# Attention by pairs of heads: scale in the queries, mask and maximum in one operation, reciprocals on a diagonal

## The reference

```python
s_nb  = einsum(q_r, k_nb) * dh**-0.5 + bias          # neighbourhood: bias, or -1e30 off the window
s_ctx = einsum(q_r, kc)   * dh**-0.5
probs = softmax(concat([s_nb, s_ctx]))
out   = einsum(probs_nb, v_nb) + einsum(probs_ctx, vc)
# windowed GQA: the same with a band mask, q heads 4g..4g+3 on kv head g, and a sink:
probs = softmax(concat([s_band, s_ctx, s_sink]))     # the sink has no value row
```

## Time and profile before

| | us |
|---|---|
| median of 3 runs | 3332.6 (3328.14 to 3336.45) |
| the profiled execution | 3334.65 |
| its span | 3332.8 |
| mean granted clock of TensorE, share of 2.4 GHz | 0.76 |
| TensorE (PE) busy | 2535.4 (76%) |
| VectorE (DVE) busy | 1962.9 (59%) |
| ScalarE (ACT) busy | 515.1 (15%) |
| GpSimd (POOL) busy | 973.9 (29%) |
| moved from HBM and to it | 1023.45 MB, mean 307 GB/s |

### The profile page before, as it was taken

The page is one execution under the profiler, slowest core; times in us unless marked ns, Lnnn a source line. Parts: engine busy times, 40 slices in busy tenths (PEclk is TensorE's granted clock), DMA queues, the critical chain, the costliest instruction groups (busy, mean ns, idle before and its releaser), DMA issues.

```text
span 3332.8 us, 32715 instructions
## 1 busy us (share of the span) xinstructions
PE 2535.4 (76%) x10880; PEld 1289.2 (39%) x10880; DVE 1962.9 (59%) x6008; ACT 515.1 (15%) x1106; POOL 973.9 (29%) x967
## 2 busy tenths in 40 slices
PE   6889983789999969658889876777988366566555
PEld 5768872243455535124444411113677011111111
DVE  4778958747544466875444455554646855555555
ACT  2151111124322111002022200001502000000000
POOL 0830000276322222323932233331000233333332
PEclk7989986695899979668889866566898555665666
DMA  7606732897899979886999999994042599989997
GB/s 301 234 29 260 300 132 112 342 380 277 349 400 377 384 297 368 323 339 256 334 388 402 410 362 398 393 401 196 26 160 95 228 372 388 407 343 403 403 405 309
DMA packets 147881, 1023.45 MB, mean 307 GB/s; under 512 B 18816, under 2 KB 19328, under 8 KB 28032
## 3 DMA queue, kind: packets, MB, share of 16 engines
q0 software_dynamic: 110592, 805.36, 60.9%
q1 hardware_dynamic: 30496, 202.36, 15.9%
q10 hardware_dynamic: 6624, 13.64, 1.1%
HBM read 1011.32 MB, written 9.96 MB: 306 GB/s over the span
## 4 chain that ended last, share of the span: by engine, by line
PE 45%; DMA 20%; DVE 19%; POOL 8%; issue 5%; ACT 3%; ACTq 0%; DVEq 0%; POOLq 0%; SPq 0%
DMA ring<-in_peer_uv,eT 20%; PE PS L1043 10%; PE PS L821 6%; DVE ring L1709 6%; POOL ring L660 5%; PE PS L978 5%; PE PS L1061 4%; PE PS L756 3%; PE PS L939 2%; PE PS L842 2%; PE PS L826 2%; PE PS L885 2%; PE PS L908 2%; DVE ring L1379 1%; POOL mix L555 1%
## 5 line engine op out<-in xcount | busy, mean ns | idle before, releaser
L1709 DVE CUSTOM_DVE_ANT_0 ring<-ring,PS 128x512 f32<-128x512 f32 x1536 | 993.2, 684 | 830.1 <-PE PS L1061 454.8
L660 POOL DMA_INDIRECT ring<-in_peer_uv,eT x768 | 726.6, 946 | 2224.0 <-PE PS L1043 1339.7
L1061 PE MATMUL PS<-xr,onesb 3*128 3x512 bf16 x1536 | 610.4, 483 | 379.1 <-DVE hcol L1709 329.1
L1043 PE MATMUL PS<-ring,zcol 128*32 128x512 f32 x3072 | 601.0, 924 | 185.9 <-DVE zcol L1719 184.6
L1061 PEld LDWEIGHTS PS<-xr,onesb 3*128 3x128 bf16 x1536 | 108.8, 96 | 959.1 <-DVE hcol L1709 474.6
L1043 PEld LDWEIGHTS PS<-ring,zcol 128*32 128x32 f32 x3072 | 104.8, 144 | 491.5 <-DVE zcol L1719 257.2
L821 PE MATMUL PS<-uT,W 128*128 128x256 f32 x1024 | 249.9, 393 | 4.3 <-issue 4.3
L1312 ACT ACTIVATE ge<-hdot 128x4 f32<-128x4 f32 x192 | 39.4, 205 | 1382.7 <-DVE hdot L1714 1371.4
L1379 DVE CUSTOM_DVE_ANT_0 ring<-ring 128x1024 f32<-128x1024 f32 x160 | 211.6, 1361 | 28.6 <-DMA ring<-in_w_rows 23.8
L821 PEld LDWEIGHTS PS<-uT,W 128*128 128x128 f32 x1024 | 193.5, 194 | 62.8 <-issue 34.7
L978 PE MATMUL PS<-uT,W 128*128 128x256 f32 x768 | 183.2, 395 | 0.0
(11 more groups left out here) (190 smaller groups left out, 2418.9 us busy)
## 6 DMA issues: line engine op xcount, KB each, us to landing
ring<-in_w_rows SPq DMA_DIRECT2D x40, 1024.0 KB, 8.0
W<-in_w_in SPq DMA_DIRECT2D x30, 1024.0 KB
W<-in_w_q SPq DMA_DIRECT2D x24, 1024.0 KB
W<-in_w_gate SPq DMA_DIRECT2D x16, 1408.0 KB
W<-in_w_gate SPq DMA_DIRECT2D x16, 1280.0 KB
W<-in_w_gate SPq DMA_DIRECT2D x16, 1024.0 KB
W<-in_w_out SPq DMA_DIRECT2D x12, 1024.0 KB
xr<-xrows ACTq DMA_DIRECT2D x768, 6.0 KB
```

Source lines behind the costliest of these rows:

```text
L660: pool.indirect_dma_start(ring[:, slot, :], None, (peer_uv0, peer_uv1)[b.l], bass.IndirectOffsetOnAxis(eT[:, f % 2, t:t + 1], 0)).then_inc ...
L1043: last = T.matmul(PS[k * NR:(k + 1) * NR, (6 + h) * 512:(7 + h) * 512], zcol[:, g % 2, k, NR - 1 - at:2 * NR - 1 - at], ring[:, slot, D + ...
L1061: T.matmul(bank(x_bank(q, n) + h), onesb[32 * k:32 * k + 3, :], xr[32 * k:32 * k + 3, g % 2, h * 512:(h + 1) * 512], start=True, stop=True)\
L1709: V.tensor_tensor_reduce(out=u_half, in0=u_half, in1=bank(x_bank(q, n) + h), scale=1.0, scalar=0.0, op0=ALU.mult, op1=ALU.add, accum_out=h ...
```

## The change

The 24 jobs become 12 of two heads each, one on each half of the partitions. The scale goes into the queries when they leave PSUM (`qcols` holds the scaled bias columns, made once at the start). `bounded` takes the place of `scaled`: one `tensor_tensor_reduce` for each 256 columns adds the mask (or a zero) and takes the row's maximum, writing the scores to `Sm` with the accumulator. `normed` no longer scales the rows; it writes the reciprocals onto two 128x128 diagonals in `stage_c` (identity times reciprocal), and `transposed` is an ordinary product of the scores with that diagonal. `Sm` is 2 pairs deep, so that `bounded(n)` waits for `transposed(n-2)`; `PT` moves to `mix`. The latent scores alternate between banks 2, 3 and 6, 7; the context's have banks 2 and 3 alone, and `scores(n+1)` there waits for the maximum of pair n. Step n holds `transposed(n-1)` and `values(n-2)`, 14 steps instead of 27, with a share of 2.0 tokens each instead of 1.2. ScalarE does `exps` ahead of `probs` and `outputs`. GpSimd issues two taps of the convolution a step. The heads of `w_branch_d` are laid out in the new order on the host.

```diff
-SHARE = {"ada": 1.0, "ln": 1.5, "unit": 0.9, "fft": 0.9, "rope": 1.2, "job": 1.2, "conv": 1.3, "gate": 1.1, "out": 0.9,
+SHARE = {"ada": 1.0, "ln": 1.5, "unit": 0.9, "fft": 0.9, "rope": 1.2, "job": 2.0, "conv": 1.3, "gate": 1.1, "out": 0.9,
...
-    return [(br, h, qt) for br, heads in ((0, NAT_H), (1, GQA_H)) for h in range(heads) for qt in range(TT)]
+    return [(br, c, qt) for br, pairs in ((0, NAT_H // 2), (1, GQA_H // 2)) for c in range(pairs) for qt in range(TT)]
...
-        Sm = part(scr, 0, [SM, 2 * TOK])
-        PT = part(scr, SM * 2 * TOK, [2 * TOK])
+        Sm = part(scr, 0, [2, 2, 2 * TOK])
+        PT = part(mix, 14 * TOK, [4 * TOK])
...
+        def s_bank(s, n):
+            return 6 if s == 0 and n % 2 else 2
...
-                for n in range(len(JOBS) + 3):
+                for n in range(len(JOBS) + 2):
+                    next(taps[b.front], None)
                     next(taps[b.front], None)
...
+                    br, c, qt = JOBS[n]
+                    at = s_bank(s, n)
+                    before = 2 if s == 0 else 1
+                    if n >= before:
+                        pe.wait_ge(a["sm"], a.at("sm", n - before + 1))
+                    rows_ = [slice(e * DH, (e + 1) * DH) for e in range(2)]
+                    of_q = (nq, gqk)[br]
...
+                        ks = [nkb[st_][:, c, :] for st_ in ((0, 1) if s == 0 else (1,))]
...
+                        ks = [gqk[:, 4, :], gkc[:, :]] if s == 0 else [gkc[:, :]]
                     for m, k_ in enumerate(ks):
-                        last = T.matmul(bank(2 + n % 2, m * TOK, (m + 1) * TOK), q_, k_, start=True, stop=True)
+                        for e in range(2):
+                            last = T.matmul(bank(at + e, m * TOK, (m + 1) * TOK), of_q[rows_[e], c, qt * P:(qt + 1) * P],
+                                            k_[rows_[e], :], start=True, stop=True)
                     last.then_inc(a["S"], 1)
...
-                    for q in range(nk):
-                        last = T.transpose(bank(4, q * P, (q + 1) * P), Sm[:, n % SM, q * P:(q + 1) * P], ident[:, :])
+                    for e in range(2):
+                        for q in range(nk):
+                            to = bank((4, 0)[e], q * P, (q + 1) * P) if s == 0 else bank(4, (2 * e + q) * P, (2 * e + q + 1) * P)
+                            last = T.matmul(to, Sm[:, n % 2, e, q * P:(q + 1) * P], stage_c[:, n % 2, e * P:(e + 1) * P],
+                                            start=True, stop=True)
                     last.then_inc(a["ptp"], 1)
...
+                        st_ = (0, 0, 1, 1)[q] if s == 0 else 1
+                        for e in range(2):
+                            if br == 0:
+                                v_ = nvf[st_][:, q % 2, (2 * c + e) * DH:(2 * c + e + 1) * DH]
+                            else:
+                                v_ = gvb[st_][:, q % 2, e * DH:(e + 1) * DH]
+                            last = T.matmul(PS[e * DH:(e + 1) * DH, 5 * 512:5 * 512 + P], v_,
+                                            PT[:, (e * nk + q) * P:(e * nk + q + 1) * P], start=(q == 0), stop=(q == nk - 1))
...
                 scores(0)
-                for n in range(len(JOBS) + 3):
+                for n in range(len(JOBS) + 2):
                     if n + 1 < len(JOBS):
                         scores(n + 1)
-                    if 2 <= n < len(JOBS) + 2:
-                        transposed(n - 2)
-                    if n >= 3:
-                        values(n - 3)
+                    if 1 <= n <= len(JOBS):
+                        transposed(n - 1)
+                    if n >= 2:
+                        values(n - 2)
...
+                        if dst[0] in ("nq", "gq"):
+                            j = dst[1] + 2 * (dst[0] == "gq")
+                            A(dst_of[dst[0]](dst[1]), bank(2 + n % 4, 0, TOK), fn, scale=SCALE, bias=qcols[:, l, j:j + 1])\
+                                .then_inc(a["unit_act"], 1)
...
                     act.wait_ge(a["sm"], a.at("sm", n + 1))
-                    last = A(Sm[:, n % SM, 0:w], Sm[:, n % SM, 0:w], ACT.Exp, bias=st8[:, q, 1:2], accum_out=st8[:, q, 2:3])
+                    for e in range(2):
+                        last = A(Sm[:, q, e, 0:w], Sm[:, q, e, 0:w], ACT.Exp, bias=st[:, q, 4 + e:5 + e],
+                                 accum_out=st[:, q, 6 + e:7 + e])
                     if br:
-                        last = A(st8[:, q, 3:4], sink[:, h:h + 1], ACT.Exp, bias=st8[:, q, 1:2])
+                        last = A(st[:, q, 8:10], st[:, q, 8:10], ACT.Exp)
...
-                    A(PT[:, 0:w], bank(4, 0, w), ACT.Copy).then_inc(a["pts"], 1)
+                    if s == 0:
+                        A(PT[:, 0:w], bank(4), ACT.Copy)
+                        A(PT[:, w:2 * w], bank(0), ACT.Copy).then_inc(a["pts"], 1)
+                    else:
...
-                for n in range(len(JOBS) + 3):
-                    if 2 <= n < len(JOBS) + 2:
-                        probs(n - 2)
-                    if n >= 3:
-                        outputs(n - 3)
+                    A(yb[:, (2, 6)[br] + c, qt * P:(qt + 1) * P], bank(5, 0, P), ACT.Copy).then_inc(a["y"], 1)
+                act.wait_ge(pch_s, gated[b.front])
+                for n in range(len(JOBS) + 2):
                     if n < len(JOBS):
                         exps(n)
+                    if 1 <= n <= len(JOBS):
+                        probs(n - 1)
+                    if n >= 2:
+                        outputs(n - 2)
...
-                def scaled(n):
...
-                    if n >= SM:
-                        dve.wait_ge(a["ptp"], a.at("ptp", n - SM + 1))
+                    if n >= 2:
+                        dve.wait_ge(a["ptp"], a.at("ptp", n - 1))
+                    go = dict(scale=1.0, scalar=LOWEST, op0=ALU.add, op1=ALU.max)
+                    none = zero[:, 0:1].to_broadcast([P, TOK])
+                    for e in range(2):
+                        if s == 0:
+                            m_ = bias[:, qt, 2 * c + e, :] if br == 0 else band[:, qt, :]
+                            ch.add(V.tensor_tensor_reduce(out=Sm[:, q, e, 0:TOK], in0=bank(at + e, 0, TOK), in1=m_,
+                                                          accum_out=st[:, q, e:e + 1], **go))
+                        ch.add(V.tensor_tensor_reduce(out=Sm[:, q, e, w - TOK:w], in0=bank(at + e, w - TOK, w), in1=none,
+                                                      accum_out=st[:, q, 2 + e:3 + e], **go))
+                    ch.wait()
...
-                        m_ = bias[:, qt, h, :] if br == 0 else band[:, qt, :]
-                        ch.add(V.scalar_tensor_tensor(Sm[:, n % SM, 0:TOK], bank(b_, 0, TOK), SCALE, m_, ALU.mult, ALU.add))
-                        ch.link(V.tensor_scalar(Sm[:, n % SM, TOK:w], bank(b_, TOK, w), SCALE, None, ALU.mult))
+                        ch.link(V.tensor_tensor(st[:, q, 2:4], st[:, q, 0:2], st[:, q, 2:4], ALU.max))
+                    if br:
+                        of_c = sink[:, c:GQA_H:GQA_H // 2]
+                        ch.link(V.tensor_tensor(st[:, q, 2:4], st[:, q, 2:4], of_c, ALU.max))
+                        ch.link(V.tensor_scalar(st[:, q, 4:6], st[:, q, 2:4], -1.0, None, ALU.mult))
+                        V.tensor_tensor(st[:, q, 8:10], of_c, st[:, q, 4:6], ALU.add).then_inc(a["sm"], 1)
                     else:
-                        ch.link(V.tensor_scalar(Sm[:, n % SM, 0:w], bank(b_, 0, w), SCALE, None, ALU.mult))
-                    ch.link(V.reduce_max(st8[:, q, 0:1], Sm[:, n % SM, 0:w], AX))
-                    if br:
-                        ch.link(V.tensor_tensor(st8[:, q, 0:1], st8[:, q, 0:1], sink[:, h:h + 1], ALU.max))
-                    V.tensor_scalar(st8[:, q, 1:2], st8[:, q, 0:1], -1.0, None, ALU.mult).then_inc(a["sm"], 1)
+                        V.tensor_scalar(st[:, q, 4:6], st[:, q, 2:4], -1.0, None, ALU.mult).then_inc(a["sm"], 1)
...
-                        ch.link(V.tensor_tensor(st8[:, q, 2:3], st8[:, q, 2:3], st8[:, q, 3:4], ALU.add))
-                    ch.link(V.reciprocal(st8[:, q, 4:5], st8[:, q, 2:3]))
-                    V.tensor_scalar(Sm[:, n % SM, 0:w], Sm[:, n % SM, 0:w], st8[:, q, 4:5], None, ALU.mult).then_inc(a["pn"], 1)
-                for n in range(len(JOBS) + 3):
+                        ch.link(V.tensor_tensor(st[:, q, 6:8], st[:, q, 6:8], st[:, q, 8:10], ALU.add))
+                    ch.link(V.reciprocal(st[:, q, 10:12], st[:, q, 6:8]))
+                    for e in range(2):
+                        last = V.tensor_scalar(stage_c[:, q, e * P:(e + 1) * P], ident[:, :], st[:, q, 10 + e:11 + e], None,
+                                               ALU.mult)
+                        if e:
+                            last.then_inc(a["pn"], 1)
+                        else:
+                            ch.add(last)
```

More of the change, by code:

```diff
@@ L260, in build @@
         ge = sb("ge", [P, 2, GRP])
-        st8 = sb("st8", [P, 2, 8])
+        st = sb("st", [P, 2, 12])
```

(2 more changed lines are left out.)

62 lines of the change are left out of this document (27 added, 35 removed).

## The result

| | before | changed |
|---|---|---|
| median of 4 runs | 3334.5 us (3328.1 to 3340.8) | 3376.4 us (3368.3 to 3379.5) |
| ratio | | 1.0121, 95% interval 1.0098 to 1.0144 |

A forecast was written before the change was run, and what follows sets the result against it. TensorE was taken to bound all three attentions before, and the wait loop through VectorE and the transposes the changed latent ones. -6.5 - 9 + 4 + 7 = -4.5 on 3334.65 gave 3330 us, median 3328; range 3303 to 3358.

The forecast's parts named there:

- Prices of a pair: Latent attention, full clock: reads 0.35 us each, transposes 1.95 to 2.05, scores 1.05 and values 1.0 with halves overlapping.
- The rivals without overlap: Products on array halves don't overlap: pairs at all (3370 us, chance 0.14) or only the values (3340 us, 0.08).
- a rival with the values at 2.0: Only the values don't overlap, TensorE's latent cycle 4.9 us, total 3340 us; chance 0.08.
- The cycle of the latent attention: Reads wait for the transposes of pair n-1, making a loop of 4.45 us, or 5.05 with a sink.
- Lead-in, half clock and tail of the latent attentions: Latent attentions: lead-in 7.4 us at full clock, tail 2.2, half clock +4.3 in the first, +5 in the third.
- -6.5: First latent attention: 68.5 us for 75.0.
- -9: Second latent attention (third of the three attentions): 68.5 us for 77.5.
- At full clock ... mean 8.3: Context attention: mean step 8.3 us at full clock for 3.5 steps, against 10.85 at half clock for 9.
- +4: Context attention: 127 us against 123, with three quarters of the time at half clock.
- "They fall into its idle time, 0" to "+7": Selection: 5 more tokens at 1.4 to 1.6 us each add 7 us, or 0 if VectorE's idle time takes them.
- The rival that ended slower: Pairs don't overlap on the array: +12 us in each latent attention, +18 in the context, total 3370 us; chance 0.14.
- The sign that was named for "wrong": Latent cycles near 5.8 or 8 us; context attention under 115 or over 140 us.

The follow-up runs named there:

- experiment 8: Changed kernel, but in the latent attentions VectorE does reciprocals and diagonals of pair n-1 ahead of the reads of pair n: 3354.3 us, ratio 1.0051.
- Experiment 7: Context attention in half steps, TensorE's next scores moved behind the first token, two pairs deep: 3351.4 for 3374.1 us; moved ahead of it, three deep: 3346.8 for 3329.0.
- share_2_3: Changed kernel with the share of a job step 2.3 instead of 2.0, putting 32 tokens into the context attention: 3367.3 us, ratio 1.0087.
- share_0: Changed kernel with the share of a job step 0, so no tokens in the context attention: 3370.2 us (one run).

## Why the prediction was wrong

It said 3330 us for the profiled execution; its own time is 3379.5, 49 us more. By its own steps:

- **Prices of a pair: right.** Reads 0.35 apart, eight scores 1.13 for 1.05, transposes 2.05 as said, sixteen values 1.09 for 1.0, and both products overlap on halves of the array. The rivals without overlap fall. The rule of the Trainium skill ("TensorEngine Tiling (Array Packing)", Key Properties) that different tiles run in parallel agrees with this trace. From the rule of the Trainium skill on weight loads ("TensorE: Matmul & The Clock Gate", Part 3, What overlaps and what doesn't) the prediction had drawn a rival with the values at 2.0; they took 1.09.
- **The cycle of the latent attention: right in its mechanism, a little low in size.** 5.30 for 5.05 in seven cycles, 4.41 in the last. It was rightly read that reads wait for transposes; experiment 8 shows it.
- **Lead-in, half clock and tail of the latent attentions: too small.** By the terms of the sum, each to the end of its transposes, for the first attention: lead-in 12.1 us for 10.4; the first three cycles 20.3 for 14.7 (13.4 and 1.3 for the half clock); the eight with a sink 41.5 for 40.4; the tail 3.6 for 2.2; and nothing apart for the taps' 0.8. That is 77.5 for 68.5. The cycles are the largest part: I took the half clock for 0.4 of a cycle, and the stretched small operations for 0.8 us once, and both stood in a loop in which nothing else could go on: the transposes of 3.78 us in the first of the three, the small operations in the last. The tail holds a copy and two rounds of values, not one. -6.5 became +2.5, -9 became -5.4: 12.6 us.
- **"At full clock ... mean 8.3", 3.5 steps of it: the step that failed in the context attention.** The figure does not follow from its own terms: with 4.2 down to 2.3 and the rest as it was, 10.85 becomes 8.95. And only one step came near either, 9.0 us at a granted clock of 0.69; those at 0.76 and 0.77 took 10.0 and 12.6. My reading is that a step that waits in turn on TensorE and VectorE gains from the clock only where TensorE works. The mean of all steps, 10.9, hits the 10.85 of the half clock, but partly by luck: without weighing they took 10.0 for 8.65, with it 11.7 for 13.05. All 12 steps at 10.9, with head and end, make 141; +4 became +17. The text named the wait and the broadcasts queued behind it, and yet priced the whole as if a quarter of it went away. Experiment 7 shows what that queue cost.
- **"They fall into its idle time, 0" to "+7": the tokens behind were too cheap.** I priced one by VectorE's busy time, 1.4 to 1.6. Five more came with a selection 18.9 us longer, 3.8 each; taken out again in share_2_3 they gave back 2.5 each. The rest of the 18.9, and the 5.4 us up to the projection, which the sum had at nothing, go with the paired steps in the attention and are not explained. So +7 became +24, 17 of the 49 us. Why a token costs more than VectorE's part in it is argued and not shown. It is an exchange between TensorE and VectorE (broadcast, dots, broadcast), whose round trip is longer than either part. The rival is its transfer: 805.36 MB for 768 tokens is 1.05 MB each, an estimated 2.5 us even at the 419 GB/s of the fastest window above, near the 2.4 and 2.5 us of share_0 and share_2_3, and the DMA share in the stages behind was 0.81 to 0.94. No run tells the two apart.
- The rival that ended slower took another mechanism (no overlap), so its 3370 is near for the wrong reason. The sign that was named for "wrong", a context attention over 140 us, is the one that came.

13 us in the context attention, 17 behind it, 13 in the latent attentions, and 6 spread over the other stages, where no cause can be told from scatter, make the 49.

## What to carry to other kernels

Where two streams of work are laid by hand into one order for in-order engines, ask of each wait what independent work stands behind it on the same engine: here moving one wait behind one token was worth 18 to 23 us of 3340 with the same instructions, and a deeper lag took another 8 to 16 us off the attention. Price a step that hands work back and forth by its round trip, and hold that against the time of its transfer; a count of one engine's busy time, or a half or full clock, said little here. A fusion that halves the number of steps also halves the number of places in which the other stream can go. But cutting the steps again gained nothing by itself (143.2 us for 141.1), nor did the depth by itself (141.9): look for the wait first. And when the fusion moves work of the other stream into a later stage, compare stages with the same amount of it.
